# Mixers of a two-part transformer: attention copies ahead of weight splits, two transposes ahead of a gate, the attention result in two parts, gated branches first

## The reference, cut to what matters

```python
def token_mixer_2(u, w_in, b_gate, attn_sink, pool_w, pool_scale, w_br_attn, w_br_pool, w_out, cos, sin):
    proj = u @ w_in
    q, k, v, p, ga, gb = jnp.split(proj, splits, axis=-1)
    q = partial_rope(q.reshape(b, s, N_HEADS, HEAD_DIM), cos, sin)
    k = partial_rope(k.reshape(b, s, N_KV_HEADS, HEAD_DIM), cos, sin)
    y_attn = windowed_gqa(q, k, v, attn_sink) @ w_br_attn
    y_pool = multiscale_pool(p, pool_w, pool_scale) @ w_br_pool
    gate_a = jax.nn.sigmoid(ga + b_gate[:D_MODEL])
    gate_b = jax.nn.sigmoid(gb + b_gate[D_MODEL:])
    return (gate_a * y_attn + gate_b * y_pool) @ w_out
```

## Time and profile before

| | |
|---|---|
| median of 3 runs | 2366.41 us (2365.16 to 2368.33) |
| the profiled execution | 2362.65 us, span of the trace 2360.8 us |
| PE busy | 1977.2 us, 84% |
| DVE busy | 1005.2 us, 43% |
| ACT busy | 667.8 us, 28% |
| mean of the DMA engines' load | 279 GB/s |
| first mixer, second mixer in the trace | about 1505 to 1637 us, about 2033 to 2165 us |

### The profile page before, as it was taken

The page is one execution under the profiler, slowest core; times in us unless marked ns, Lnnn a source line. Parts: engine busy times, 40 slices in busy tenths (PEclk is TensorE's granted clock), DMA queues, the critical chain, the costliest instruction groups (busy, mean ns, idle before and its releaser), DMA issues. The chain is left out here.

```text
span 2360.8 us, 27246 instructions
## 1 busy us (share of the span) xinstructions
PE 1977.2 (84%) x11690; PEld 1367.8 (58%) x11690; DVE 1005.2 (43%) x1284; ACT 667.8 (28%) x739; POOL 9.3 (0%) x6
## 2 busy tenths in 40 slices
PE   6999986666666776666664999989999999989998
PEld 3888773222222222222221888888888888888887
DVE  6667461000000000000002667557777767567766
ACT  4444230000000000000002334554434434554433
POOL 1000000000000000000000000000000000000000
PEclk9999997888887777788887999999999999999999
DMA  8362667999999999999999445434454555434542
GB/s 352 129 245 91 246 273 336 432 430 434 429 434 431 430 434 428 435 431 431 433 428 386 157 182 195 180 128 155 182 198 176 211 198 190 179 116 160 196 180 98
DMA packets 34089, 659.70 MB, mean 279 GB/s; under 512 B 3784, under 2 KB 4296, under 8 KB 6224
## 3 DMA queue, kind: packets, MB, share of 16 engines
q1 hardware_dynamic: 31984, 650.55, 67.5%
q10 hardware_dynamic: 2016, 7.84, 0.9%
HBM read 657.34 MB, written 1.05 MB: 279 GB/s over the span
## 5 line engine op out<-in xcount | busy, mean ns | idle before, releaser
L1477 PE MATMUL ps<-u_both,w_hi 128*128 128x512 f32 (+1 forms) x1792 | 545.2, 364 | 0.0
L1232 DVE TENSOR_TENSOR ring_lo<-ring,w_hi 128x2048 fp32r<-128x2048 f32 x168 | 384.7, 2291 | 225.7 <-ACT w_hi L656 225.6
L1477 PE MATMUL ps<-u_both,ring_lo 128*128 128x256 f32 x1536 | 430.7, 280 | 0.0
L656 ACT CAST w_hi<-ring 128x2048 fp32r<-128x2048 f32 x168 | 320.0, 1905 | 226.0 <-PE ps L1477 224.9
L1477 PEld LDWEIGHTS ps<-u_both,w_hi 128*128 128x128 f32 x1792 | 319.8, 188 | 58.5 <-issue 0.7
L1477 PEld LDWEIGHTS ps<-u_both,ring_lo 128*128 128x128 f32 x1536 | 290.1, 189 | 1.6
L1477 PE MATMUL ps<-ring_b,area_h 128*32 128x512 f32 x1024 | 161.6, 794 | 80.5 <-DMA ring_b<-experts_dram 72.0
L1477 PE MATMUL ps<-ring,area_h 128*32 128x512 f32 x1024 | 158.2, 781 | 72.0 <-DMA ring<-experts_dram 64.2
L1222 DVE TENSOR_TENSOR expert_area<-expert_area,ps 128x512 f32<-128x512 f32 x16 | 11.0, 688 | 453.3 <-PE ps L1477 453.3
L635 ACT COPY expert_area<-ps 128x1024 f32<-128x1024 f32 x16 | 16.2, 1012 | 616.1 <-PE ps L1477 616.1
L1212 DVE TENSOR_TENSOR area_h<-ps,mod 128x256 f32<-128x256 f32 x16 | 6.8, 425 | 393.2 <-PE ps L1477 393.2
(11 more groups left out here) (358 smaller groups left out, 2390.4 us busy)
## 6 DMA issues: line engine op xcount, KB each, us to landing
ring<-stream_dram SPq DMA_DIRECT2D x115, 2048.0 KB, 7.8
ring_b<-experts_dram SPq DMA_DIRECT2D x48, 4096.0 KB, 31.0
ring<-experts_dram SPq DMA_DIRECT2D x48, 4096.0 KB, 31.0
area_n<-norm_rows_dram ACTq DMA_DIRECT2D x6, 512.0 KB, 4.5
x_tok<-x_dram SPq DMA_DIRECT2D x2, 1024.0 KB, 8.6
tail<-filt_out_dram SPq DMA_DIRECT2D x1, 1536.0 KB, 6.7
tables<-tabs_dram ACTq DMA_DIRECT2D x1, 1408.0 KB, 6.9
tabs<-tabs_dram ACTq DMA_DIRECT2D x1, 1296.0 KB, 16.2
```

The source lines that it names most:

```text
L656: A.copy(upper_part(n), ring[:, n % RING, :]).then_inc(sig("alone_hi_ready") if n in ALONE else sig("w_hi_ready"), 1)
L1232: V.tensor_tensor(ring_lo[:, n % RING, :], ring[:, n % RING, :], upper_part(n).bitcast(F32), ALU.subtract).then_inc(sig("alone_ready") if ...
L1477: ins = M.matmul(out, lhsT, rhs, start=start, stop=stop, **more)
```

## The change

Five things move in both mixers.

- DVE: `keep_att(0)` moves ahead of `scores(1)`, and `keep_att(2)` ahead of the split of MIX_AT + 12.
- PE: `turn_att(4)` and `turn_att(5)` move ahead of `gate(7)`. ACT's `keep_att(5)` moves ahead of its `gate(7)`, and its `upper` of MIX_AT + 15 goes behind `keep_att(7)`.
- PE: the first branch product on `mixT` goes ahead of the attention products, the second behind them.
- The attention result goes over in two parts, one for each bank: two CASTs and two subtractions of 128x512 for one of 128x1024, with a semaphore each.
- The branches from k = 2 on wait for `gated` (DVE has read the bank, L1441) where they waited for `mT_ready` (DVE has made the sum too).

```diff
@@ ACT
-                    upper(l, MIX_AT + 8 + k)
+                    if k < 7:
+                        upper(l, MIX_AT + 8 + k)
...
+                keep_att(5)
                 gate(7)
-                keep_att(5)
                 keep_att(7)
-                act.wait_ge(sig("a2T_ps"), l + 1)
-                A.copy(a2T[:, 0], ps[:, 0:2, :].rearrange("p b (j t) -> p (b j) t", j=2)).then_inc(sig("a2T_hi"), 1)
+                upper(l, MIX_AT + 15)
+                for b in range(2):
+                    act.wait_ge(sig("a2T_ps"), l * 2 + b + 1)
+                    A.copy(a2T[:, 0, 2 * b:2 * b + 2, :],
+                           bank(b).rearrange("p (j t) -> p j t", j=2)).then_inc(sig("a2T_hi"), 1)
@@ DVE
                 lower(l, MIX_AT + 11)
+                keep_att(0)
                 scores(1)
+                keep_att(2)
                 lower(l, MIX_AT + 12)
-                keep_att(0)
-                keep_att(2)
                 lower(l, MIX_AT + 13)
                 probabilities(1)
...
-                dve.wait_ge(sig("a2T_hi"), l + 1)
-                V.tensor_tensor(a2T[:, 1], ps[:, 0:2, :].rearrange("p b (j t) -> p (b j) t", j=2),
-                                a2T[:, 0].bitcast(F32), ALU.subtract).then_inc(sig("a2T_ready"), 1)
+                for b in range(2):
+                    j = slice(2 * b, 2 * b + 2)
+                    dve.wait_ge(sig("a2T_hi"), l * 2 + b + 1)
+                    V.tensor_tensor(a2T[:, 1, j, :], bank(b).rearrange("p (j t) -> p j t", j=2),
+                                    a2T[:, 0, j, :].bitcast(F32), ALU.subtract).then_inc(sig("a2T_ready"), 1)
                 for k in range(KD):
                     dve.wait_ge(sig("branch2_ps"), l * KD + k + 1)
                     g = sgate[:, k, :, :].rearrange("p g t -> p (g t)")
-                    step(V.tensor_tensor(g, bank(6 + k % 2), g, ALU.mult))
+                    V.tensor_tensor(g, bank(6 + k % 2), g, ALU.mult).then_inc(sig("gated"), 1)
+                    dve.wait_ge(sig("gated"), KD + l * KD + k + 1)
@@ PE
+                turn_att(4)
+                turn_att(5)
                 gate(7)
-                for c in range(4, 8):
-                    turn_att(c)
+                turn_att(6)
+                turn_att(7)
+
+                def branch(k, g):
+
+                    w = split(MIX_AT + 13 + k // 2)
+                    if k >= 2 and g == 1:
+                        pe.wait_ge(sig("gated"), KD + l * KD + k - 1)
+                    for i in range(4):
+                        if k == g == 0 and i % 2 == 0:
+                            pe.wait_ge(sig("a2T_ready"), l * 2 + i // 2 + 1)
...
+                pe.wait_ge(sig("mixT_ready"), l + 1)
+                pe.wait_ge(sig("gate_kept"), l * KD + KD - 1)
+                branch(0, 1)
...
-                               ready=sig("a2T_ps") if j == 3 and f == k == 1 else None)
-                pe.wait_ge(sig("mixT_ready"), l + 1)
+                               ready=sig("a2T_ps") if j % 2 == 1 and f == k == 1 else None)
                 pe.wait_ge(sig("gate_kept"), l * KD + KD)
-                for k in range(KD):
-                    w = split(MIX_AT + 13 + k // 2)
-                    if k >= 2:
-                        pe.wait_ge(sig("mT_ready"), l * KD + k - 1)
...
+                branch(1, 1)
+                branch(0, 0)
+                branch(1, 0)
+                for k in range(2, KD):
+                    branch(k, 1)
+                    branch(k, 0)
```

More of the change, by code:

```diff
@@ L2114, in _ @@
                        ready=sig("mixed_ps") if g == 3 else None)
+                turn_att(4)
+                turn_att(5)
                 gate(7)
-                for c in range(4, 8):
-                    turn_att(c)
+                turn_att(6)
[7 more added lines that the diff above has]
+                            pe.wait_ge(sig("a2T_ready"), l * 2 + i // 2 + 1)
+                        y = (a2T, mixT)[g]
+                        a = (k % 2) * 1024 + g * 512 + i * P
+                        last = g == 0 and i == 3
+                        product3(bank(6 + k % 2)[:, g * T:(g + 1) * T], [v[:, a:a + P] for v in w],
+                                 (y[:, 0, i, :], y[:, 1, i, :]), i == 0, i == 3,
+                                 free=int(last and k % 2 == 1), ready=sig("branch2_ps") if last else None)
+                pe.wait_ge(sig("mixT_ready"), l + 1)
+                pe.wait_ge(sig("gate_kept"), l * KD + KD - 1)
+                branch(0, 1)
                 pe.wait_ge(sig("attT_kept"), l * 4 + 4)
```

## The result

| | before | the change |
|---|---|---|
| median | 2365.78 us (2362.90 to 2368.33, 4 runs) | 2344.07 us (2342.96 to 2346.28, 4 runs) |
| ratio to before | | 0.9908, 95% interval 0.9897 to 0.992 |
| profiled execution | 2362.65 us, span 2360.8 | 2343.74 us, span 2341.8 |
| PE busy | 1977.2 us | 1968.8 us |

The change is faster by 21.7 us in the medians and by 18.9 in the profiled executions.

A forecast was written before the change was run, and what follows sets the result against it. PE, busy 84% of the span, was taken as the bound. Gains of 8.3 and 10.0 us in the mixers, 18.3, less 1.7 for one clock fall, gave 16.6: median from 2366.41 to 2349.8 us, range 2346.0 to 2355.0.

The forecast's parts named there:

- Copies ahead of the splits: DVE in the mixers: turns 2 and 3 start 3.4 us earlier, at 2086.8; 16 pooled products take 3.06 us.
- The waits that replace them: New PE waits: 0.95 us at the mixed products (ACT's pooled copy), 1.9 at turn 4 (DVE's normalization).
- gate(7): PE matmuls after turns 4 and 5, from 2102.0 to 2107.9; copies 4 and 5 hide under them.
- First branch, `a2T`, loop: Mixers' end: no wait at the attention products, a2T or the branch loop, where both waits of 0.9 us go.
- The sum without the clock: Gain of 8.3 us in the second mixer and 10.0 in the first, together 18.3 with the clock always high.
- The clock: One fall of PE's clock in the two mixers, at gate(7), costing 1.7 us of the gain; chance 0.35.
- the middle case: Three waits at the turns (3.05 of 4.85 us): the clock fell after them in the first mixer, not the second.
- Rival 1: No fall of the clock in either mixer: gain 18.3 us, time 2348.1; chance 0.25.
- Rivals 2 to 5: Falls in both mixers 2351.5 (0.17); loop waits stay 2353.4 (0.12); attention chain later 2355.8 (0.06); low clock lasts, slower 2382.5 (0.03).

The follow-up runs named there:

- e6: The change with DVE's probabilities(1) ahead of the split of MIX_AT + 13; median 2343.08 us, ratio to before 0.9903.
- e1: The kernel before with only the DVE copies keep_att(0) and keep_att(2) moved; median 2353.65 us, ratio to before 0.9956.
- e5: The change with DVE's copies 0 and 2 back behind scores(1) and the split; median 2356.73 us, ratio to before 0.996.
- e10: The change plus five unused DVE copies ahead of probabilities(1); 797.5 us from the first mixer's first transpose to the end, 7.6 more than the change.
- e3: The change with the branches waiting for mT_ready again in place of gated; median 2352.11 us, ratio to before 0.9945.
- e8: The change with all attention products ahead of the first branch again, a2T still in two parts; median 2348.69 us, ratio to before 0.9924.
- e9: The change plus two unused DVE copies ahead of probabilities(1); 791.7 us from the first mixer's first transpose to the end, 1.8 more than the change.
- e7: e6 with ACT's CAST of MIX_AT + 13 also moved behind the pooled result's copy; median 2340.50 us, ratio to before 0.9891.

## Why the prediction was wrong, point by point

- **Copies ahead of the splits**: right. Turns 2 and 3 start at once; moved to the time scale of before (10.6 us later) at 2086.8, as forecast. The pooled products take 3.27 us, not 3.06 (that came from a pair of starts of other matmuls).
- **The waits that replace them**: right in place and releaser, and in size within 0.35 us. At the mixed products I had 0.95 with the tail of the last matmul and it is 2086.82 - 2086.22 = 0.6; at turn 4 I had 1.9, and without the wait the mixed products would take 1.83 (e6: 2088.79 - 2086.96), so it is 2090.39 - 2086.82 - 1.83 = 1.7. Turn 4 starts at 2101.0 on the old scale, forecast 2101.1. That the move of turns 4 and 5 is thereby a loss of its own, 2.5 us, stood in the walk's numbers, and I didn't draw it out: I priced the whole and not that part against leaving it out.
- **gate(7)**: 2097.04 - 2091.24 = 5.8 us, forecast 5.9.
- **First branch, `a2T`, loop**: right; no wait at any of them. The attention products start at 2110.0 on the old scale, forecast 2110.2, the output product at 2135.3, forecast 2135.5. The two edits are worth 1.4 and 5.4 us when undone alone.
- **The sum without the clock**: 8.3 and 10.0 us forecast, 8.5 and 10.1 measured. The 0.5 us between the mixers weren't forecast. 18.3 against 19.0.
- **The clock: the step of the mechanism that failed.** I charged one fall, 1.7 us, "nearest to the middle case", and it was none. The Trainium skill's section ("TensorE: Matmul & The Clock Gate", "A second HAM failure mode: psum-queue depth-cycling"), which I had weighed beside it, tells of short idles in one kernel; taken as a rule it would have made two falls here, 3.4 us. The trace of the changed kernel doesn't agree, with 1.00 in all windows, nor does e1 at the three waits of its turns. The middle case itself was one execution's: e1 has the same three waits twice and no fall. I read that group as if it decided. Nor would the length of a wait have decided: 1.57 us stands next to the 1.35 of that group and far from the 3.26 after which the clock had always fallen, but at 296 us in the first block it fell after 1.93 in two profiles. What the runs show is that after 0.45 and 1.57 us it fell in none of ten mixers. Rival 1, no fall, was the case; it had 0.25.
- **The range: the term that put the time outside.** From the forecast to the measured median are 5.7 us: 1.7 for the fall that didn't come, 0.7 that the stretch brought beyond the case without a fall, 2.7 by which the medians' gain (21.7) exceeds the stretch's (19.0), and 0.6 by which the median of before lay lower in this comparison. The range already held the case without a fall, 2348.1, and went 2 us below it, by the spread of three runs' times. That allowance was too small: the change's median is 2344.07 in one comparison and 2349.08 in two others, 5.0 apart, by falls of the clock in the first block that the edits don't touch. Had either of the two others been the result, it would have lain 0.7 us from the forecast, and that would have been luck, with the clock's term as wrong as it is.
- **Rivals 2 to 5** fell: no low clock, no loop wait, and the attention chain of DVE and ACT was, if anything, 0.1 us early.

What stays open: why the three waits at the turns preceded a fall in one mixer of four, and what makes the clock fall at 296 and 347 us of the first block in some executions and not in others, which moves the mixers by up to 8 us.

## What to carry to other kernels

Walk the one engine that bounds through all edits together, since what one edit wins the next wait takes: the copies were worth 10.9 us alone (1.7 of them a fall of the clock that may have been chance) and 6.5 in company, and one of the parts cost 2.5. Where a wait is left, look whether its releaser stood behind work that itself was waiting for something; moving small work with a waiting consumer ahead of bulk work for later slots brought 5 us more, without a new wait. Where the parts of a program that an edit doesn't touch scatter by more than the effect, measure from a landmark ahead of the edit to the end: that repeated within 0.4 us where the medians differed by 5.

## What the runs showed of the hardware

- In the mixers, idle times of PE of 3.26 and 3.27 us (before, e5) and of 3.88 and 3.89 (e10) were followed by the low clock in all six mixers; the pair of 0.45 and 1.57 (the change three times, e3, e8) and that of 0.46 and 2.50 (e9) in none of twelve. One fall cost 1.5 to 2.95 us.
- The length of one idle time alone doesn't decide. At 294 us of the first block PE stood idle for 1.93 to 2.80 us and the clock fell to 0.50 in nine profiles; it stood idle for 1.97 to 2.33 and the clock stayed at 1.00 in five (before, the change, e1, e6, e7).
- The same idle time doesn't cost the same: after 3.27 us the transposes and pooled products of e5's first mixer lost 1.7 us, after 3.26 those of the second 2.95. By windows of 1 us the clock was low from about 1569.5 to 1573 us in the first and from about 2088.4 to 2095.2 in the second, twice as long.
- A bracket understates a wait by the tail that it uncovers: 0.73 us in a bracket at the loop cost 0.9, 0.45 at the mixed products 0.6. In e8 a bracket of 0.77 cost 0.7 all the same, in a changed order.
